# A two-block transformer step: the HGRN recurrence and the convolutions placed between the tiles of the first input product

## The reference, cut to what matters

```python
mod = silu(c) @ w_ada + b_ada                      # six vectors: shift, scale, gate (mixer), the same (ffn)
sh_m, sc_m, gt_m, sh_f, sc_f, gt_f = jnp.split(mod[:, None, :], 6, axis=-1)
h = rmsnorm(x, pre_mix_norm) * (1.0 + sc_m) + sh_m
proj = h @ w_in                                    # 2048 x 8208: q f i g | q k v g | a b
o_hg = hgrn2_group(proj[..., :HG_COLS], lb, hg_norm)
o_gdn = gdn_group(proj[..., HG_COLS:], conv_w, a_log, dt_bias, gdn_norm)
y = jnp.concatenate([o_hg, o_gdn], axis=-1) @ w_out
x = x + gt_m * rmsnorm(y, post_mix_norm)
...
# hgrn2_group: f = lb + (1-lb) sigmoid(f_logit); k = 1 - f; v = i
#   S_t = diag(f_t) S_{t-1} + k_t v_t^T,  o_t = S_t^T q_t
#   o = rmsnorm(o, norm_w) * silu(g_out)
# gdn_group: qkv = silu(causal_conv(p[..., :3072], conv_w))      (4 taps, one weight per channel)
#   q, k normalised per head; log_a, beta from the 16 columns a, b
#   S_t = a_t S_{t-1}(I - beta_t k_t k_t^T) + beta_t k_t v_t^T,  o_t = S_t^T q_t
#   o = rmsnorm(o, norm_w) * silu(g_out)
```

## Time and profile before

| | us |
|---|---|
| median of 3 runs | 3159.67 (3142.24 to 3160.5) |
| the profiled execution | 3148.27 |
| its span | 3146.6 |
| mean granted TensorE clock | 0.947 of full |
| PE, PEld, DVE, ACT, POOL busy | 2875.1, 2781.6, 1939.2, 1305.6, 337.8 |

### The profile page before, as it was taken

How to read it: one execution, slowest core, us unless ns; L and a number is a source line. 1 busy time by engine, 2 the same in 40 slices (tenths; PEclk the granted TensorE clock), 3 DMA queues, 4 the chain that set the end, 5 groups by cost and what they waited for, 6 DMA issues and landing times. The chain is left out here.

```text
span 3146.6 us, 56575 instructions
## 1 busy us (share of the span) xinstructions
PE 2875.1 (91%) x22467; PEld 2781.6 (88%) x22467; DVE 1939.2 (62%) x2712; ACT 1305.6 (41%) x2040; POOL 337.8 (11%) x492
## 2 busy tenths in 40 slices
PE   2299999768899999999999999999899999999998
PEld 2299998657898999999999998888799999999998
DVE  5866665756467556666676757767447654444554
ACT  1244444252344444443443445455534343333444
POOL 2011111800001111111111002222001100000000
PEclk6599999778999999999999999999999999999999
DMA  8587876110174778767777367666448755554553
GB/s 321 217 266 247 264 255 197 54 54 1 65 252 162 258 267 273 268 235 252 251 241 251 127 177 237 205 199 209 145 135 292 268 180 184 183 186 161 183 179 134
DMA packets 280099, 632.14 MB, mean 201 GB/s; under 512 B 24770, under 2 KB 45702, under 8 KB 279686
## 3 DMA queue, kind: packets, MB, share of 16 engines
q1 hardware_dynamic: 223696, 467.97, 44.5%
q0 software_dynamic: 44800, 159.41, 15.1%
q10 hardware_dynamic: 11446, 2.54, 0.5%
HBM read 627.77 MB, written 2.10 MB: 200 GB/s over the span
## 5 line engine op out<-in xcount | busy, mean ns | idle before, releaser
L987 PE MATMUL accumulators<-h_parts,weight_parts 128*128 128x256 f32 x5696 | 1445.3, 286 | 14.3 <-DVE weight_parts L903 14.3
L989 PE MATMUL accumulators<-h_parts,weight_parts 128*128 128x256 f32 x5696 | 1441.7, 285 | 0.0
L903 DVE TENSOR_TENSOR weight_parts<-weights,weight_parts 128x1024 fp32r<-128x1024 f32 (+1 forms) x840 | 878.8, 1059 | 594.7 <-ACT weight_parts L843 592.4
L987 PEld LDWEIGHTS accumulators<-h_parts,weight_parts 128*128 128x128 f32 x5696 | 1104.6, 194 | 20.5 <-DVE weight_parts L903 20.4
L843 ACT ACTIVATE weight_parts<-weights 128x1024 fp32r<-128x1024 f32 (+1 forms) x840 | 754.4, 924 | 877.2 <-PE accumulators L989 372.5
L989 PEld LDWEIGHTS accumulators<-h_parts,weight_parts 128*128 128x128 f32 x5696 | 1104.9, 194 | 0.0
L980 PE MATMUL accumulators<-h_parts,weight_parts 128*128 128x256 f32 x5696 | 933.0, 286 | 54.6 <-ACT weight_parts L843 29.7
L980 PEld LDWEIGHTS accumulators<-h_parts,weight_parts 128*128 128x128 f32 x5696 | 795.9, 194 | 62.0 <-issue 18.1
L370 DVE SCALAR_TENSOR_TENSOR ada_sums<-ada_weights,c_act,ada_sums 128x512 f32<-128x512 f32 x336 | 241.1, 744 | 0.0
L2150 PE MATMUL accumulators<-in_h_parts,in_weight_parts 128*128 128x256 f32 x1632 | 218.9, 289 | 7.2 <-ACT wide L2204 3.2
L2150 PEld LDWEIGHTS accumulators<-in_h_parts,in_weight_parts 128*128 128x128 f32 x1632 | 205.5, 194 | 17.1 <-issue 7.0
(11 more groups left out here) (352 smaller groups left out, 2053.4 us busy)
## 6 DMA issues: line engine op xcount, KB each, us to landing
weights<-in_w_ff SPq DMA_DIRECT2D x128, 1024.0 KB, 6.3
weights<-in_w_in SPq DMA_DIRECT2D x80, 1024.0 KB, 7.1
ada_weights<-in_w_ada POOLq DMA_DIRECT2D x96, 512.0 KB, 6.0
h_t<-in_ada_w POOLq DMA_DIRECT2D x96, 512.0 KB, 5.9
weights<-in_ffn_w_gate SPq DMA_DIRECT2D x44, 1024.0 KB, 5.2
weights<-in_ffn_w_up SPq DMA_DIRECT2D x44, 1024.0 KB, 5.2
weights<-in_ffn_w_down SPq DMA_DIRECT2D x44, 1024.0 KB, 5.0
ada_weights<-in_w_ada SPq DMA_DIRECT2D x64, 512.0 KB, 8.0
```

The costliest lines, as they stand in the source:

```text
L903: ins = nc.vector.tensor_tensor(w[:, held:held + take, 1, :], core.ring[:, q % RING, k:k + take, :], w[:, held:held + take, 0, :].bitcast( ...
L987: nc.tensor.matmul(accs[nt], w[:, held, 0, cols[nt]], xk[:, 1, :], start=False, stop=False, skip_group_check=True)
L989: ins = nc.tensor.matmul(accs[nt], w[:, held, 1, cols[nt]], xk[:, 0, :], start=False, stop=(last and nt % 2 == 1), skip_group_check=True)
```

## The change

1. The column groups of `in_1` come in the order f, q (HGRN), q, k, v (GDN), i, g (HGRN), g (GDN): `COLUMN_ORDER`.
2. `phase_in_1` takes the place of `phase_split_product` for this stage and of `phase_hgrn`. All 256 slots are written out; the HGRN work and all three convolutions are issued at given slots. A level starts every 15 slots from slot 78; v, outputs and mean squares follow from slot 199.
3. The convolutions are wholly on POOL, head by head (7 instructions a head, each waiting for the one before), into `hT`. They can start when a column group is evicted: at slot 98 for q. ACT's Silu on them stands at slots 144, 194 and 242, and POOL's part 1 waits for the first Silu, part 2 for the eighth level's differences.
4. The ada weights of `in_1` go through SP, in 2 slots instead of 4, between the loads of the product's weights; ACT evicts the first half of a turn's tiles while PE works on the second half.
5. The eight groups of the mid ada chunks (`ada_mid`, now `ada_gdn`) move from HGRN to GDN: two after the squares, three before the wait for `nt_ready`, three at the end, where 12 idle products are left of 44. GDN also takes the Silu of its own gate, and builds three of the masks on POOL at its start (before: in the setup stage).

```diff
+COLUMN_ORDER = [HF // HH, HQ // HH, GQ // HH, GK // HH, GV // HH, HI // HH, HG // HH, GG // HH]
...
+AFTER_REFILL = {2: (2, 3), 3: (4,), 4: (5,), 5: (6, 7), 6: (8,), 7: (9,)}
+LEVEL_SLOT, LEVEL_SLOTS = 78, 15
...
+            ada.first_loads(sp)
+            for g in range(RING, st.groups):
+                i, q = g // st.unit, g % st.unit
+                refill(sp, core, st, i, q)
+                for n in AFTER_REFILL.get(q, ()):
+                    if i + n // st.unit < st.turns:
+                        ada.load_when_free(sp, i + n // st.unit, n % st.unit)
+            prefetch(sp, core, core.streams["ada_gdn"])
...
+            for part, first in ((0, 0), (1, 0), (2, HH)):
+                if part == 1:
+                    pool.wait_ge(s["conv_act"], 1)
+                if part == 2:
+                    pool.wait_ge(s["diff_ready"], NL)
+                evicted(pool, GQ + part * HH)
                 for j in range(HH):
...
+                    nc.gpsimd.tensor_scalar(to, src, weight(3), None, ALU.mult)
+                    for tap in (2, 1, 0):
+                        back = 3 - tap
+                        core.pool.link(pool, nc.gpsimd.tensor_scalar(tapped[:, back:SEQ], src[:, 0:SEQ - back],
+                                                                     weight(tap), None, ALU.mult))
+                        ins = nc.gpsimd.tensor_tensor(to[:, back:SEQ], to[:, back:SEQ], tapped[:, back:SEQ], ALU.add)
+                        core.pool.link(pool, ins)
+                pool.sem_inc(s["convolved"], 1)
...
+            def level(l):
+                yield from pace.until(level_slot(l) + 3)
+                act.wait_ge(s["diff_ready"], l + 1)
+                nc.scalar.activation(X[:, l % 2, :], X[:, l % 2, :], ACT.Exp).then_inc(s["exp_ready"], 1)
...
+            def silu(part, first, slot):
+                yield from pace.until(slot)
+                act.wait_ge(s["convolved"], part + 1)
+                nc.scalar.activation(flat(GQ + part * HH, HH), hT[:, first:first + HH, :].rearrange("p a b -> p (a b)"),
+                                     ACT.Silu).then_inc(s["conv_act"], 1)
...
+                if i and slot % TILES in (0, 2):
+                    empty(i - 1, slot % TILES // 2)
+                pace.at(slot)
...
+                yield from pace.until(level_slot(l))
...
+                nc.vector.tensor_tensor(x0, ref, b0, ALU.subtract)
+                yield from pace.until(level_slot(l) + 1)
...
+                yield from pace.until(level_slot(l) + 6)
+                dve.wait_ge(s["exp_ready"], l + 1)
                 nc.vector.tensor_tensor(x0, x0, k0, ALU.mult)
+                yield from pace.until(level_slot(l) + 7)
+                nc.vector.tensor_tensor(x1, x1, q1, ALU.mult).then_inc(s["prod_ready"], 1)
+                if l:
+                    for n in range(4):
+                        yield from pace.until(fill_slot(l, n) + 5)
...
+            step_slot = lambda i, n: 2 + 3 * n // 2 if i else 5 + 5 * n // 4
...
@@ phase_gdn, PE
+            modulation(0, 1)
             pe.wait_ge(eg_ready, 2)
...
+            modulation(2, 3, 4)
             pe.wait_ge(nt_ready, 1)
...
-            keep_warm(nc, core, pe, 44)
+            modulation(5, 6, 7)
+            keep_warm(nc, core, pe, 12)
...
-        phase_split_product(nc, core, "in_1", "ada_mid", on("act", into(core.big)), ada=[(w_ada, 0, 8, 1)])
-        with nc.sbuf_tensor("convolved", [P, 3 * HH, SEQ], F32) as conv:
-            phase_hgrn(nc, core, conv)
-            phase_gdn(nc, core, conv)
+        phase_in_1(nc, core, [(w_ada, 0, 8, 1)])
+        phase_gdn(nc, core)
```

702 lines of the change are left out of this document (406 added, 296 removed).

## The result

| | before | after |
|---|---|---|
| median of 4 runs, us | 3157.82 | 3083.06 (3082.08 to 3086.37) |
| ratio | | 0.9772, 95% interval 0.9748 to 0.9797 |
| span of the profiled execution | 3146.6 | 3082.2 |
| mean granted TensorE clock | 0.947 | 0.955 |

The forecast was 3082. The total agrees to 1 us, but two of its terms don't: both were 20 to 24 us wrong, in opposite directions, so the agreement of the total is luck. The stage borders show it. These are timeline rows of the changed kernel (start, length, engine, line): first product of `in_1`, first instruction of GDN, first product of `out_1`.

What follows compares the result with a forecast made beforehand. PE was taken to bound the input product, and HGRN to be a chain from engine to engine. Terms: -142.1 + 58.9 - 10.8 + 33 - 5 = -66 us, from 3148.3 to 3082; range 3042 to 3124.

Steps and rivals of the forecast that it cites:

- HGRN as a stage, its PE work, evictions: HGRN's stage goes, -142.1 us; its PE work enters the input product, +58.9; PE's waits for evictions there vanish, -10.8.
- DVE in the levels, +33: Product stage, slots 98 to 202: DVE becomes the bound beside POOL; with bursts and transfers +33 us, bounds 0 and +75.
- PE alone: Slots 98 to 202: 105 slots at 1.51 us and seven levels at 3.82 need 185 us of PE.
- POOL against DVE, 40 us: Levels: POOL's convolutions cost DVE 40 us, raising it to 192 us against PE's 185, so 7 us lost.
- Bursts, 18 us: First two slots of each level: DVE falls about 3 us behind PE; 2.6 us lost per level, 18 in all.
- Transfers, 8 us: Product stage: weight loads lag where DVE lags, since a load waits for DVE's earlier group; 8 us, bounds 0 and 20.
- POOL's pace: Convolutions in the product stage: POOL takes 10 us a head, 80 a part, just in time; nothing added.
- Rival (b): Product stage: POOL is late at 14 us a head and ACT stands at its Silu; -24 us, 3124; chance 0.10.
- (c): Levels: every POOL instruction shuts DVE out for its whole length; -22 us in total, 3126; chance 0.06.
- (d): Product stage, slots 78 to 255: PE's clock falls; slower from a 0.22 half-clock share, 3201 at 0.4; chance 0.05.
- GDN, -5: GDN stage: head -6.8, rows' broadcast -5, middle groups +1.2, end +5.1; sum -5 us, bounds -14 and +8.
- Two ada groups keep PE active: GDN, ahead of the rows' broadcast of 14.00 us: two groups keep PE active, saving 5 us, bounds 0 and -7.

Runs made afterwards that it cites:

- both halves: Against the changed kernel: ACT empties both halves of the banks together after the fourth tile of the next turn, as before the change; 3090.8 us.
- one tap: Against the changed kernel: POOL does only the last of four taps of each convolution, leaving 24 of 168 instructions; 3072.6 us.
- light levels: Against the changed kernel with 128-column modulation products in GDN: 45 instead of 59 ada steps within the levels, load order also changed; 3061.7 us.
- chunks on DVE: Against the changed kernel: modulation chunks 16 and 17 leave GDN and are summed on DVE beside the product, 160 ada steps; 3064.0 us.

## Why the prediction was right in its total and wrong in two steps

**HGRN as a stage, its PE work, evictions: right.** The stage's excess over PE alone (446.3) is 13.3 us, and PE's waits for DVE and ACT in it are 12.5 (9.0 + 3.5). With POOL nearly silent 6.1 of the 13.3 remain (452.4), outside the levels. Evictions are shown by both halves.

**DVE in the levels, +33: 13.3.** The mechanism holds (PE waits for the low part, only beside POOL), the size was more than double the measured one. Term by term:

- *DVE alone* was right: 152 us for 105 slots is 139.0 for 96, and one tap shows 138.84.
- *PE alone* was set too high. I took 1.51 us a slot as a mean over the stage. It carries the stage's start: the first 32 slots took 63.8 us in the change. In the levels the true value gives 163 for 96 slots.
- *POOL against DVE, 40 us*: 21.5 in 96 slots (160.29 - 138.84; up to 27.4 in other executions of this code), against 36.6 expected for 96. The 0.54 a head came from the one case where DVE stood through a whole long instruction of POOL. In the interleaved kernel DVE's operations are short and many, a two-input instruction of POOL costs 0.34 and a one-input one 0.10, half of the 0.2 that the prediction had taken.
- *Bursts, 18 us*: nothing by themselves. With POOL silent the bursts are all there, and PE is busy 162.81 of 163.10 us. Only together with POOL is there a loss, 9 to 13 us in the levels. What less work on DVE gives back (light levels) isn't clear of the spread; where levels are dense DVE is the bound and each costs 0.6 us.
- *Transfers, 8 us*: nothing in the levels by the same row. Where ada steps stand one to a slot they bind: slots 64 to 79 took 5.6 us more (chunks on DVE).

**POOL's pace, Silu, masks: right**, as the rows above show. Rival (b) did not come, nor (c), nor (d) in the product stage.

**GDN, -5: +18.8.** This step failed. The head gave its 7 us: the second Exp of the norms begins 16.7 us after GDN's start instead of 23.8 (rows of after, then of before).

```profile
616.30 1.90 ACT L1615 ACTIVATE gdn_work<-gdn_work 128x2048 f32<-128x2048 f32 x1
```

```profile
707.21 1.89 ACT L1387 ACTIVATE gdn_work<-gdn_work 128x2048 f32<-128x2048 f32 x1
```

But then:

- *Groups at 3.63 for 32 instructions* was the wrong one of two rows. The trace of before had the reason. These are the windows over the two rows:

```profile
580.27:587.10 6.83, 6.82 (x33) 6.74 (x32) 6.59 (x3) 1.69 (x2) 6.73 (x3) 0.50 0.00 1
594.26:597.89 3.63, 3.63 (x34) 3.54 (x32) 3.43 (x2) 0.00 (x0) 3.55 (x2) 1.00 0.00 0
```

  The same group costs 6.83 us at a clock of 0.50 and 3.63 at 1.00. Before, a level's 128-column products followed each group; in the trains of the change most instructions ran at 0.50. Eight groups are 47.9 us instead of 29.0.
- *"Two ada groups keep PE active"* is the statement that fell. They keep it busy and leave its clock at 1.2 GHz, so the broadcast stays at 14.00. Groups 2 to 4 add what has no wait to hide in. Together +8.6 us at DVE's take, where I had -10.6.
- *At the end* 20.2 us stand where 9.99 stood: +10.2, not +5.1.

I had the slower row, and used it as a bound for the middle place only. Used for all three it would have given -6.8 + 0 + 10.8 + (20.5 + 2.7 - 10.0) = +17, and that should have been the upper bound of the term instead of +8. That it comes so near to the measured 18.8 is again in part luck: the second and the third train cost less than 6.83 a group, as they began at the full clock.

The Trainium skill, "TensorE: Matmul & The Clock Gate", section "What's actually happening", says that the gate is set by how busy the array has recently been. If busy is read as the busy time in the profile, the rows here don't agree: with PE filled to 7.00 of 7 us the clock is 0.50 with one column and 1.00 with 128. How much of that time the array itself was at work the profile doesn't tell.

**The start, -3.1,** was forecast as nothing. The executions of unchanged code there begin `in_1` at 140.0 to 141.7 us, so part of it is scatter; the rest I haven't taken apart. It is open, as is whether relief of DVE in the levels gives PE more than the spread between executions.

## What to carry to other kernels

Before PE work is put into a stage of chains, read the granted clock of that work where it stands in a train, and not where it alternates with wide products: the price can be double. A narrow product that stands in such a train can be made wide: here that halved its time. When DVE and POOL run side by side, price POOL's cost from many short operations, and count one-input and two-input instructions apart. And a total that comes out right says little: compare the stages.

## What was not expected of the hardware

- Products of 128x128 weights with one column took 0.213 us an instruction at a granted clock of 0.50, with PE busy without a pause; with 128 columns 0.114 at 1.00. Two trains of one column began at 1.00 and fell to 0.50 after 2.4 and 4.9 us. With 64 columns the clock rose from 0.50 to 1.00 within the first group, and went back to 0.50 by the groups behind a wait for weights.
- The broadcast of the rows (a stationary side of 8 partitions, 512 columns) ran at a mean clock of 0.64 right behind groups that had held 1.00, and took 11.04 us; behind 40 idle products 9.27; behind groups of one column or a pause 14.00.
- DVE lost 0.10 us beside a one-input instruction of POOL of 1.4 us, and 0.34 (up to 0.45 by other executions) beside a two-input one of 1.0 us.
- The median landing time of the ada weights rose from 4.7 to 6.3 us when a quarter more of them was loaded in the same stage (chunks on DVE).
